# Weight tiles split by ScalarE and VectorE, the output stage joined to the layer's last steps, and the sample recurrences moved to the convolution steps

## What is computed

```python
h = rmsnorm(x, g_pre)
p = h @ w_in                        # 3344 columns, shared among four groups
a_out = c_b * conv3(c_c * c_x) * silu(c_z)                 # A: short convolution, 256 wide
b_out = rmsnorm(gla(g_q, g_k, g_v, decay), gla_g) * silu(g_z)   # B: gated linear recurrence, 4 heads
c_out = window_attention(s_q, s_k, s_v, sinks) * silu(s_z) # C: window 128, rotary, 4 q / 2 kv heads
d_out = memory_attention(m_q, mem_k, mem_v) * silu(m_z)    # D: 256 memory tokens, 4 heads
x = x + rmsnorm(concat(a_out, b_out, c_out, d_out) @ w_out, g_post)
```

## Time and profile before

| | us |
|---|---|
| median of 3 runs | 2118.95 |
| lowest, highest | 2116.91, 2126.06 |
| profiled execution, its time | 2123.05 |
| profiled execution, its span | 2120.9 |

### The profile page before, as it was taken

One profiled execution on the slowest core, in us unless ns is written; L12 is line 12 of the kernel. 1 busy time (PEld: TensorE's weight loads), 2 busy tenths in 40 slices (PEclk: granted clock), 3 DMA queues, 4 the chain that ended last, 5 costly groups with the idle time before them and its releaser, 6 DMA issues. The chain is left out here.

```text
span 2120.9 us, 42798 instructions
## 1 busy us (share of the span) xinstructions
PE 1978.8 (93%) x16314; PEld 1121.9 (53%) x16314; DVE 1276.0 (60%) x2845; ACT 880.4 (42%) x2175; POOL 332.2 (16%) x251
## 2 busy tenths in 40 slices
PE   9999899989999998898999997998999999889998
PEld 4455444444566665565544544443546666555633
DVE  5577765665356755555646786566645676645533
ACT  4554343543444332343445543344435452332322
POOL 1444323000000000000124343320100000000000
PEclk9999999999999999999999998999999999999999
DMA  7732244656521133354365232546563113234532
GB/s 263 179 99 57 66 120 120 149 171 205 132 57 32 51 84 88 95 132 150 136 160 137 70 85 66 144 117 180 167 194 71 62 52 74 51 96 106 139 113 89
DMA packets 327495, 241.66 MB, mean 114 GB/s; under 512 B 188631, under 2 KB 273117, under 8 KB 327261
## 3 DMA queue, kind: packets, MB, share of 16 engines
q1 hardware_dynamic: 324180, 228.34, 39.4%
q10 hardware_dynamic: 3112, 10.59, 1.6%
HBM read 136.60 MB, written 57.71 MB: 92 GB/s over the span
## 5 line engine op out<-in xcount | busy, mean ns | idle before, releaser
L2021 PE MATMUL bank<-h_hi,w_parts 128*128 128x512 f16 (+4 forms) x4240 | 837.9, 344 | 40.4 <-ACTq L2409 17.3
L2021 PEld LDWEIGHTS bank<-h_hi,w_parts 128*128 128x128 f16 (+1 forms) x4240 | 401.5, 98 | 392.9 <-issue 86.5
L2021 PE MATMUL bank<-h_lo,w_parts 128*128 128x512 f16 (+3 forms) x2160 | 439.5, 345 | 0.8
L2021 PEld LDWEIGHTS bank<-h_lo,w_parts 128*128 128x128 f16 (+1 forms) x2160 | 206.9, 98 | 180.0 <-issue 16.7
L3147 PE MATMUL bank<-scr_h,tb_h 128*128 128x512 f16 x768 | 179.3, 393 | 15.0 <-ACT tb_h L2431 9.9
L3147 PE MATMUL bank<-w_parts,tb_h 128*128 128x512 f16 x768 | 170.3, 379 | 1.6 <-DVEq L3295 1.6
L2408 ACT ACTIVATE tb<-bank 128x512 f32<-128x512 f32 (+1 forms) x140 | 71.9, 514 | 224.8 <-PE bank L2021 210.1
L2977 POOL TENSOR_SCALAR w_raw<-w_raw 128x1024 f32<-128x1024 f32 x46 | 132.3, 2883 | 76.8 <-DMA w_raw<-in_w_in 76.1
L2543 ACT ACTIVATE bank<-bank,stat 128x256 f32<-128x256 f32 x256 | 113.7, 446 | 58.7 <-DVE stat L2906 58.4
L3147 PEld LDWEIGHTS bank<-scr_h,tb_h 128*128 128x128 f16 x768 | 76.8, 101 | 109.0 <-issue 15.0
L2972 POOL TENSOR_TENSOR w_parts<-w_raw,w_parts 128x1024 f16<-128x1024 f32 x46 | 101.4, 2207 | 206.1 <-ACT w_parts L2381 205.3
(11 more groups left out here) (339 smaller groups left out, 2718.3 us busy)
## 6 DMA issues: line engine op xcount, KB each, us to landing
w_in_kept<-w_parts SPq DMA_DIRECT2D x104, 256.0 KB, 3.1
w_parts<-w_in_kept SPq DMA_DIRECT2D x104, 256.0 KB, 2.9
w_raw<-in_w_in SPq DMA_DIRECT2D x48, 512.0 KB, 4.3
out<-scr SPq DMA_DIRECT2D x32, 512.0 KB, 2.6
scr<-in_x_prompt SPq DMA_DIRECT2D x16, 512.0 KB, 4.1
scr<-out SPq DMA_DIRECT2D x16, 512.0 KB, 4.2
rot<-out ACTq DMA_DIRECT2D x12, 512.0 KB, 3.8
mix_t<-in_x_prompt SPq DMA_DIRECT2D x8, 512.0 KB, 11.7
```

The costliest lines, as they stand in the source:

```text
L2021: m = mm(bank[b][0:m_w, 0:c1 - c0], w[:, k, 0:m_w], h[:, k, c0:c1], start=it["piece"] == 0 and k == 0, stop=it["piece"] == 2 and k == KT - 1)
```

## The change

GpSimd no longer touches weight tiles: `wscale` is gone, ScalarE's split waits for the DMA and has the scale as its factor, VectorE makes the low part with scale and subtraction in one instruction. `conv_out` takes no engine: SP waits for VectorE and stores the transposed state by the DMA's own strides, once for each unit. The sample recurrences become side jobs of A0's two slots, and the sample buffers are dealt anew. C's second halves may join in second passes too, and begins of slots with nothing but A don't wait. In the out stage TensorE begins with the first product when its own two banks are free and counts up `left` behind it; ScalarE's and VectorE's first steps and the order list's head are changed; `o_mix` waits for fewer slots and for A1's first gate.

```diff
-SAMPLE_ROW = {("D", 0): 0, ("B", 0): 1, ("B", 1): 2, ("C", 0): 0, ("A", 0): 1, ("C", 1): 0, ("D", 1): 1, ("A", 1): 0}
+SAMPLE_ROW = {("D", 0): 0, ("B", 0): 1, ("B", 1): 2, ("C", 0): 0, ("A", 0): 0, ("C", 1): 1, ("D", 1): 2, ("A", 1): 0}
...
-            main = ("C", st["g"], 0) if st["unit"] == "B" else (st["unit"], st["g"], 1)
+            main = ("A", 0, st["g"]) if st["unit"] == "B" else (st["unit"], st["g"], 1)
...
-        return s["st"] == 1 and (s["unit"] == "D" or s["unit"] == "C" and not with_sample)
+        return s["st"] == 1 and s["unit"] in "CD"
...
-                main.append(item("begin", slot=x["index"], steps=[x["main"]] + x["side"], joined=False))
+                free = x["main"]["unit"] == "A" and all(s["unit"] == "A" for s in x["side"])
+                main.append(item("begin", slot=x["index"], steps=[x["main"]] + x["side"], joined=free))
...
+        if not mixed[0] and ended >= len(slots) - 3 and ("evict", slots[-2]["main"]["n"], "z") in placed:
+            emit(item("o_mix"))
+            mixed[0] = True
...
+        if with_sample and (ev["unit"], ev["role"]) == ("A", "x") and ev["last"]:
+            for st in groups[ev["group"]]:
+                if st["st"] != 0:
+                    emit(item("conv_out", step=st))
...                                                     # SP
+                elif it["kind"] == "conv_out":
+                    s = it["step"]
+                    g, sample = s["g"], s["st"] == "s"
+                    sp.wait_ge(u_done, conv_steps.index(s["n"]) + 1)
+                    dst = of_layer((conv_s if sample else conv_p).rearrange("l b t d -> l (b t) d"), l)[:, P * g:P * g + P]
+                    sp.dma_start(dst.rearrange("t p -> p t"), conv_st_t[:, g] if sample else conv_tail[:, g]).then_inc(stored, 16)
...                                                     # ScalarE
-                    act.wait_ge(w_scaled, t - RING + 1)
+                    act.wait_ge(raw_in[t % RING], need[t])
...
-                    fn(hi_of(t), w_raw[:, t % RING, :, 0:split_width(t)], ACT.Copy).then_inc(w_hi_done, 1)
+                    fn(hi_of(t), w_raw[:, t % RING, :, 0:split_width(t)], ACT.Copy, scale=W_UP).then_inc(w_hi_done, 1)
...
-                    all_steps_done(act, n_slots - 1)
+                    all_steps_done(act, n_slots - 3)
+                    gate_written(act, next(x["n"] for x in plan["steps"] if (x["unit"], x["g"], x["st"]) == ("A", 1, 0)))
...                                                     # VectorE
+                elif kind == "wlow":
+                    t = it["tile"]
+                    if t < RING:
+                        continue
+                    dve.wait_ge(w_hi_done, t + 1)
+                    stt(lo_of(t), w_raw[:, t % RING, :, 0:split_width(t)], W_UP, hi_of(t), ALU.mult, ALU.subtract).then_inc(w_lo_done, 1)
...                                                     # GpSimd
-                    tt(lo_of(t), w_raw[:, t % RING, :, 0:split_width(t)], hi_of(t), ALU.subtract).then_inc(w_lo_done, 1)
...
-                    nc.gpsimd.tensor_scalar(raw, raw, W_UP, None, ALU.mult).then_inc(w_scaled, 1)
...                                                     # out stage
-        order = [("xn", 0), ("mix", 1), ("o", 0, 0), ("h", 0), ("xn", 1)] + [("split", i) for i in late]
-        order += [("o", 1, 0), ("h", 1), ("xn", 2), ("o", 0, 1), ("fin", 0), ("mix", 2), ("o", 1, 1), ("h", 2), ("xn", 3), ("fin", 1), ("mix", 3)]
+        first_o = ("o", 0, 0)
+        order = [("mix", 1), ("xn", 0), ("o", 0, 0), ("xn", 1)] + [("split", i) for i in late] + [("o", 1, 0), ("h", 0), ("h", 1)]
+        order += [ ("xn", 2), ("o", 0, 1), ("fin", 0), ("mix", 2), ("o", 1, 1), ("h", 2), ("xn", 3), ("fin", 1), ("mix", 3)]
...
+                    if x == first_o:
+                        for b in range(2, 4):
+                            pe.wait_ge(bank_free[b], plan["uses"][b])
...
+                    if x == first_o:
+                        for b in range(4, 8):
+                            pe.wait_ge(bank_free[b], plan["uses"][b])
+                        pe.drain().then_inc(left["pe"], 1)
...
-                        for e in ("pe", "dve"):
-                            act.wait_ge(left[e], no)
+                        act.wait_ge(left["dve"], no)
...
-            if build is not None:
-                dve.wait_ge(pre_in, 16)
-                link(ts(pre_g, pre_g, H_UP, None, ALU.mult))
...
+                    if u == 0:
+                        dve.wait_ge(pre_in, 16)
+                        link(ts(pre_g, pre_g, H_UP, None, ALU.mult))
```

More of the change, by code:

```diff
@@ L252, in place @@
         elif k == "wsplit":
-            at[("hi", it["tile"])] = run("ACT", 1.06, when(("scaled", it["tile"])))
+            at[("hi", it["tile"])] = run("ACT", 1.06, when(("raw", it["tile"])))
         elif k == "wlow":
             if not it["ready"]:
-                at[("lo", it["tile"])] = run("POOL", 2.4, when(("hi", it["tile"])))
+                at[("lo", it["tile"])] = run("DVE", 1.25, when(("hi", it["tile"])))
         elif k == "proj":
@@ L394, in place @@
             run("PE", 0.9 if unit == "C" else 1.1, self.needs(it))
-        elif k in ("conv_out", "swa_out", "conv_in", "layer_in"):
+        elif k == "conv_out":
+            self.issue(2, when(("conv", n)))
+        elif k in ("swa_out", "conv_in", "layer_in"):
             p = run("PE", 0.4, self.needs(it))
@@ L440, in last_reader @@
             return ("evict", n, "z"), u
-        return ("conv_out", n, 0) if with_sample and u["st"] != 0 else ("evict", n, "x"), u
+        return ("evict", n, "x"), u
     reader = {"B": dict(q=("gla_p", n, end), k=("gla_p", n, end), v=("gla_t", n, end - 1), z=("gla_norm", n, 0)),
@@ L531, in work @@
         if kind == "A":
-            if with_sample and st != 0:
-                out.append(item("conv_out", [2], step=s))
-        elif kind == "B":
+            return out
+        if kind == "B":
             chunks = 1 if sample else ST // CH
@@ L791, in rload @@
         fc.issue(len(tiles[t]), fc.t["PE"])
[L792 to L797, removed]
+        fc.at[("raw", t)] = fc.t["PE"] + RAW_US
     def wsplit():
         t = landing.pop(0)[1]
-        while raws and raws[0][1] <= t:
-            wscale()
         emit(item("wsplit", tile=t, ready=t < RING, after=last_use.get(t - RING)))
@@ L886, in plan_units @@
                 emit(item("o_x"))
-            if ended == len(slots) - 1:
-                emit(item("o_mix"))
             continue
@@ L1252, in stores_of @@
         if it["kind"] == "conv_out":
-            return int(it["step"]["g"] == 1)
+            return 1
         if it["kind"] == "gla_sq":
@@ L1469, in units @@
         lr = low[0:2 * RANK + 1]
-        out_c = low[64:80, 0:4 * P].rearrange("p (i g n) -> p i g n", i=2, g=2)
         o, _ = STAGE["in"]
@@ L2041, in on_tensor @@
                 elif kind == "end":
-                    if it["slot"] == n_slots - 1:
-                        for b in range(2, 8):
-                            pe.wait_ge(bank_free[b], plan["uses"][b])
-                        pe.drain().then_inc(left["pe"], 1)
-                    else:
-                        pe.drain().then_inc(step_pe, 1)
-                elif kind == "conv_out":
-                    s = it["step"]
-                    u = tile_row(s, row_of(s, "x"))
-                    pe.wait_ge(u_done, conv_steps.index(s["n"]) + 1)
-                    emptied(pe, it, 2)
-                    if s["st"] == "s":
-                        m = nc.tensor.transpose(bank[2][0:2 * NB, 0:P], conv_st_t[:, s["g"], :], ident[:])
-                    else:
-                        m = nc.tensor.transpose(bank[2][0:2, 0:P], u[:, ST:ST + 2], ident[:])
-                    m.then_inc(bank_full[2], 1)
+                    pe.drain().then_inc(step_pe, 1)
                 elif kind == "gate":
@@ L3123, in on_tensor @@
         def on_tensor(pe):
-            for x in order:
+            for i, x in enumerate(order):
                 if x[0] == "o":
@@ L3186, in on_scalar @@
                     if t == 1:
[L3188 to L3189 removed]
+                        act.wait_ge(left["dve"], no)
                     if t >= 2:
[L3191 removed]
+                        for n in range(2):
+                            act.wait_ge(out_full[out_bank(t, n)], t // 2)
                     fn(m_hi[:, t % 2, :, 0:out_size(t)], mix_t[:, :, tcols(tile_at[t])], ACT.Copy, scale=M_UP).then_inc(mh_done, 1)
@@ L3255, in on_vector @@
                     if t >= 2:
-                        dve.wait_ge(out_full[out_bank(t, 1)], t // 2)
+                        for n in range(2):
+                            dve.wait_ge(out_full[out_bank(t, n)], t // 2)
                     m_low = m_lo[:, t % 2] if r == P else m_hi[:, t % 2, :, r:2 * r]
```

47 lines of the change are left out of this document (12 added, 35 removed).

## The result

The changed kernel takes 2151.8 us (median, 2146.3 to 2155.5) against 2119.15: a ratio of 1.0146, 95% interval 1.0113 to 1.0180. The forecast was 2086 (2060 to 2116). The profiled execution took 2153.85 us, 30.8 more than that of before.

What follows compares the result with a forecast made beforehand. TensorE, busy 93% of the span, was taken as the bound, gains coming from its idle time and clock. Terms -14.7 - 4 - 2 - 12 + 0 = -32.7 from 2123.05 gave 2090.4, less 4.1 against the median: 2086 us (2060 to 2116).

Steps and rivals of the forecast that it cites:

- Part 5: Convolution state stores in second passes: -0.6 and +0.6 a pass, so 0; the load at the end is not moved.
- So 2304 fill the 16 engines for 2.5 us: Stores' 4-byte pieces for each half, priced at 17 ns a packet like 256 B ones; twice that at worst, 5 us.
- Strided stores stay in flight: Rival, slower: stores land late, delaying SP's semaphore reset; 2136 at ten times the packet price, 2212 at 47 us; chance 0.03.
- Part 2: Weight tiles in first passes: VectorE gains low parts, GpSimd's relief stands against it; -2 a pass, -4.
- At the second the low part now stands in VectorE's own queue: At the factor products ahead of the 4.0 us wait for L2744: low part costs 1.2 us, against a like relief.
- Part 1: Ends of first passes: split wait -9.9, clock -3.4, h(0) -1.4, together -14.7 us.
- part 3: A steps without handshake: begins no longer wait for all engines; -2 for both first passes, bounds -4 and 0.
- Nothing stands between 431.2 and the product: End of the first pass: the wait before the first output product goes, -9.9 us over passes 1 and 3.
- -1.4 for h(0): Behind the first output product: 3.4 us waits for h(0)'s transposes go, 1 us kept in each of two passes.
- Part 4: Second passes, sample recurrences beside A0 and joined C steps: -6 a pass, -12; bounds -19 to +16 a pass.
- A0's projections stall on C0: Rival, slower: projection banks wait for C0's second half if C0 ends later than 812; 2130, chance 0.07.
- VectorE did not become the bound: Rival: VectorE bounds the first passes, weight tiles +24.6 instead of -4, 2115; chance 0.10 with other mixtures within 0.5%.

Runs made afterwards that it cites:

- e1: Changed kernel with the convolution state stores writing each partition's values side by side (whole pieces) instead of 4-byte strided pieces: 2103.3 us, 0.9911.
- e3: Changed kernel with the convolution states turned by TensorE, copied by ScalarE and stored in whole rows as before: 2100.0 us, 0.9908.
- e6: Kernel before with the weight tiles alone changed, the planner still counting and placing a low part by GpSimd's time: 2106.5 us, 0.9942.
- e7: Kernel before, work unchanged, with only the planner's two figures changed (low part as 1.25 us of VectorE, placed by VectorE's time): 2144.7 us, 1.0127.
- e15: Kernel before with the new stage ends and the A steps without handshake, sample recurrences where they were: 2118.2 us, 0.9990.
- e5: Kernel before with sample recurrences beside A, A steps without handshake and new stage ends; weight tiles and stores as before: 2090.9 us, 0.9864.
- e11: Kernel before with the ends of the stages alone changed (early split, new output order, divided waits): 2125.0 us, 1.0037.
- e17: Changed kernel with states through TensorE, a low part booked on GpSimd and placed by VectorE's time, new ends kept; a repeat run: 2086.3 us, 0.9843.
- e4: Kernel before with the weight tiles alone changed, including the planner's new figures: 2130.5 us, 1.0046.

## Why the forecast was wrong, step by step

Measured parts: -2.1 (ends and A steps), +9.8 (weight tiles), -26.7 (sample recurrences), +50.4 (stores), together +31.4, against +30.9 measured.

- **Part 5, the stores: this failed, by 50 us.** The step was "So 2304 fill the 16 engines for 2.5 us", from the 17 ns of a packet of 256 B. I priced a write by the time of its packet, and as a bound 5 us in front of a weight load or of D1's transposition. The runs show 50 us for the 9216 writes (e1, e3), paid by the transfers behind them. The rival "Strided stores stay in flight" had that mechanism, and 2136 for ten times the packet's price; I gave it 0.03, because the only row I had was one of another size. That its 50 us are the measured 50 is luck: it had 25 at A0 and nothing at a pass's end, where only the reset of the semaphores was thought to wait; measured are 8 at A0 and 14 to 18 at the end, where D1's transposition stood right behind the store and its product started 24 us after it (966.93, 990.83). The Trainium skill (VectorE: DVE Perf Modes, The three transpose paths) compares such a copy with the hardware's transposition, 19 times slower; my 47 us put its 19 on the packets' 2.5 us. No run here shows 47, but the sign and the warning were right.
- **Part 2, the weight tiles: forecast -4, measured +9.8.** The trade on the engines was better than forecast (-12.3 in e6). What failed was a step that I did not make: a planner orders the queues, and its durations changed with the edit. "At the second the low part now stands in VectorE's own queue" looked at instructions where they stood in the trace of before; they stand elsewhere in the new plan. The two figures alone cost 27 us on unchanged work (e7).
- **Part 1, ends: forecast -14.7, measured -2.1 with part 3.** By the table of passes e15 is 7.4 us shorter than before in the two first passes with their output stages, and 3.9 us longer in the two second ones, where I had put nothing; why these grew is open. "Nothing stands between 431.2 and the product" held only together with part 3, which I had priced at -2 apart. Then -1.4 for h(0) failed: I assumed x issued 2.5 us earlier, and the scale behind x was issued 5.7 us after the start of the last attention product in e5 (438.10), against 5.1 before (435.39). In the changed kernel the wait for the split was also replaced by one for D1's probabilities, 4.4 us:

```profile
439.69 1.49 PE L2313 MATMUL bank<-rot_h,mem_v 128*64 128x256 f16 x12 [4.40 <-DMA rot_h<-rot_h]
```

 There the product came 9.4 us later than in the earlier trace rows. The wait is 4.4 in e3 too, so it isn't the stores'; e11, e15 and e17, planned otherwise, have 0.8.
- **Part 4, sample recurrences: forecast -12, measured -26.7.** The mechanism was right and the size too small; the bound of -19 a pass held. C0's second half started at 781, before the 785 I asked for (it was 801.5), and C0 ended near 807, so the rival "A0's projections stall on C0" never came to its point of 812:

```profile
781.34 0.49 PE L2257 MATMUL bank<-rot,tb 64*128 64x128 f32 x4
...
805.93 0.86 PE L2305 MATMUL bank<-w_raw_h,spare_h 128*64 128x128 f16 x24 [0.80 <-DMA w_raw_h<-w_raw_h]
```

- **The rest.** Without the stores and with the old costs the four parts make 2083 to 2086, near the forecast's 2086 by luck, for two errors cancel: -2 and -27 where I had -17 and -12. VectorE did not become the bound (261.8 us of 392.5 busy in a first pass).

## What to carry to other kernels

Price a store with tiny pieces by what stands behind it in every queue, not by its packets, and where the trace holds no write of that size, give the bad case a real chance. In a kernel whose queues a planner orders, a change of a duration is a change of its own: price it apart, and try it apart. A wait removed at a stage's end pays only if no other arrives there with it; ask of each what it hid.

## What the runs showed of the hardware

- Writes of 4 B to memory with rows 1 KiB apart cost this kernel 5.4 to 6.1 ns each (50 us and 56 us for 9216, 29.3 for 5120). Their own packets don't show it: behind the store at 818.49, 893 of them in 1.6 us keep the 16 engines 25.1% busy. Writes of 8 B with the same 1 KiB between rows cost nothing measurable (4608: 2.6 us above whole pieces, with intervals of 3.5 and 4.1 each side).

```profile
q1 hardware_dynamic: 893, 0.00, 25.1%
```

- The price is paid by others: in the 10 us from 980 the changed kernel's DMA engines stand over fully busy with 1723 packets, 73 GB/s, and the transposition among them took 20.9 us to land; the same took 4.5 us in e1. Whoever reads only the rows of the stores finds nothing.

```profile
DMA packets 1723, 0.73 MB, mean 73 GB/s; under 512 B 1643, under 2 KB 1643, under 8 KB 1723
...
q1 hardware_dynamic: 1723, 0.73, 120.4%
...
rot_h<-rot_h SPq DMA_TRANSPOSE x1, 20.9
```

- Loads of instructions were slow as well: a packet of 16 KB took 7.5 us at 834.9 and 11.5 us at 969.2, behind the stores; in e1 the one at 832.8 took 0.9.

- GpSimd's work on weight tiles slowed VectorE by 24 us a first pass, as estimated: 56.3 us of new work raised its busy time by 7.8 us in the changed kernel and by 5.9 in e4, where no other work is changed.
